# Differential attention with its units in twos, joint small steps, maxima written negated and lambda made in the query projection

## The chip, the cores and the metric

The kernel runs on one core of one Trainium2 chip. The metric is the device time of one execution in microseconds (us), the median over the runs. Five engines work side by side, each through its own queue of instructions in order: TensorE (PE in the profile, with its weight loads as PEld), VectorE (DVE), ScalarE (ACT), GpSimd (POOL) and SyncE (SP), which here issues the transfers. They wait for each other by semaphores, which the program writes out by hand.

## What is computed

The reference is two blocks of two layers each. The first has a convolution layer, a layer of differential attention, and a product-key expert layer behind each; the second has two attention layers of other kinds and two MLPs. The change touches the differential attention alone and the query projection ahead of it:

```python
def diff_attention(h, wq, k, v, lq1, lk1, lq2, lk2, subln_g, wo, lam_init, pos):
    q = (h @ wq).reshape(B, L, N_HEADS, 2, HEAD_DIM)
    q = partial_rope(q, pos) * (HEAD_DIM ** -0.5)
    lam = (jnp.exp(jnp.sum(lq1 * lk1)) - jnp.exp(jnp.sum(lq2 * lk2)) + lam_init)
    ...
        s = jnp.einsum('bqhcd,bkhcd->bhcqk', qblk, k).astype(jnp.float32)
        s = jnp.where(mask, s, -jnp.inf)
        p = jax.nn.softmax(s, axis=-1)
        a = p[:, :, 0] - lam * p[:, :, 1]
        return jnp.einsum('bhqk,bkhe->bqhe', a.astype(v.dtype), v)
    ...
    o = rmsnorm(o, subln_g) * (1.0 - lam_init)
    return o.reshape(B, L, N_HEADS * V_DIM) @ wo
```

There are 8 heads with two maps each, a head dimension of 64, values of 128, 256 tokens that ask (two tiles of 128) and 272 keys (16 meta tokens ahead of them). Each head's two score maps get a softmax of their own, and the second is subtracted with the factor lambda.

## The kernel before, in words

Matrix products in float32 precision are made from three products of rounded parts: the high part of the weights by the high part of x, high by low, low by high (`three`, L854). The weights stream from memory into a ring; ACT rounds them to a high part (`split_hi`, L546) and DVE makes the remainder (`split_lo`, L553), in halves of a chunk, four halves ahead of PE.

The stages follow each other in one list. Around the change these are `kv_proj`, `q_proj`, `diff_attn` and `proj_add`. In the query projection (8 chunks of 128 outputs, one for each head) PE projects chunk m and then multiplies the raw chunk m - 1 by a rotation matrix (`rotate`, L1231). ACT copies the raw chunk out of PSUM (L1882) and rounds the finished chunk m - 2 (`one`, L1890). DVE adds the sine part (L2569, L2571), POOL makes the cosine part (L3021) and the low part of the rounded chunk (L3027). Behind the last chunk ACT makes the two exponentials for lambda (`diff_lambda`, L1915) and DVE three small steps from them (L2605 to L2607).

The attention has 16 units u: token tile 0 with its 8 heads (144 keys), then tile 1 (272 keys). For a unit
- PE (`scores`, L1468, L1470) makes both score maps, six products and two for the causal mask, in banks 0 and 1 or 2 and 3;
- DVE (`maxima`, L2763, L2764) takes the row maxima and multiplies them by the negated scale;
- ACT (`exps`, L2058) makes both exponentials with row sums;
- DVE (`mix`, L2769 to L2773) makes reciprocals, the ratio, and the difference of the two maps;
- PE (`turn`, L1478) transposes the difference, ACT stores it (`store`, L2067), PE multiplies by the values (`weigh`, L1488) in bank 6 or 7;
- DVE (`keep_out`, L2779) scales and stores the output, ACT sums its squares (`square_sum`, L2074).

On each engine the steps of several units are interleaved in an order written out by hand: PE does `scores(u)`, `turn(u - 2)`, `weigh(u - 3)`, ACT `store(u - 2)`, `exps(u)`, `square_sum(u - 3)`, DVE `maxima(u)`, `mix(u - 1)`, `keep_out(u - 3)`. At the end ACT loads the table for the root and takes it (L1560, L2086), DVE inverts and scales the outputs (L2790, L2796), PE transposes them (L1509), and ACT and DVE make the high and low parts (L2089, L2800) that the output projection reads.

PE's clock is held up by products that nobody reads (`keep_warm`, L887): 20 ahead of the first scores and 6 behind each of the first three, 256 columns each. PE is given these by count, not by time. Which pattern of columns a call reads hangs on its count too: calls of 14 and of 20 products take the next pattern from a list that all later stages share.

Of the kernel before, what the change touches and what calls it, by code (L numbers as in the profile page):

```python
# [99 lines left out]
WARM_DIFF, WARM_FILL = 20, 6  # L100
# [94 lines left out]
def build_program(nc, dram, spill, meta_dram, out):  # L195
    stages = lay_out_stages()
    with ExitStack() as ctx:
# [148 lines left out]
        probs = av(3, 2, T0)  # L346
# [79 lines left out]
        row_max = small[:, 8:14].rearrange("p (a m) -> p a m", a=3)  # L426
        neg_max = small[:, 16:22].rearrange("p (a m) -> p a m", a=3)
        row_sum = small[:, 24:30].rearrange("p (a m) -> p a m", a=3)
# [421 lines left out]
        def _(pe):  # L850
# [29 lines left out]
            def keep_warm(n, bank=7):  # L880

                src = gated_all[:, 48:48 + SEQ]
                if n in (WARM_SCALE, WARM_DIFF):
                    parts, at = next(by_scale, (2, 48))
                    src = in_lines(at, parts)
# [570 lines left out]
            def attend_diff(s):  # L1456
# [17 lines left out]
                def turn(u):  # L1474
                    pe.wait_ge(maps_mixed, u + 1)
                    for kt, (k0, kn) in enumerate(diff_unit(u)[3]):
                        at = kt * P
                        mm = pe.transpose(banks[0:kn, 4 + u % 2, at:at + P], probs[:, u % 3, 0, k0:k0 + kn], ident)  # L1478
# [13 lines left out]
                keep_warm(WARM_DIFF)  # L1492
                pe.wait_ge(v_kept, NC)
                pe.wait_ge(masks_rounded, 1)
                for u in range(n_units + 3):
                    if u < n_units:
                        scores(u)
                    if u < 3:
                        keep_warm(WARM_FILL)
                    if 2 <= u < n_units + 2:  # L1500
                        turn(u - 2)
                    if u >= 3:
                        weigh(u - 3)
# [49 lines left out]
        def _(act):  # L1553
# [362 lines left out]

            def nsa_proj(s):
# [131 lines left out]
            def attend_diff(s):  # L2049
                n_units = NT * HEADS  # L2050

                def exps(u):
                    nk = diff_unit(u)[2]
                    act.wait_ge(max_ready, u + 1)
                    if u >= 3:
                        act.wait_ge(turned, u - 2)
                    for c in range(2):
                        ins = act.activation(probs[:, u % 3, c, 0:nk], banks[:, 2 * (u % 2) + c, 0:nk], ACT.Exp,  # L2058
                                             bias=neg_max[:, u % 3, c:c + 1], scale=SCALE, accum_out=row_sum[:, u % 3, c:c + 1])
# [16 lines left out]
                for u in range(n_units + 3):  # L2076
                    if 2 <= u < n_units + 2:
                        store(u - 2)
                    if u < n_units:
                        exps(u)  # L2080
# [1168 lines left out]
```

## Time and profile before

| | us |
|---|---|
| median of 3 runs | 2752.08 |
| lowest, highest | 2749.27, 2756.12 |
| the profiled execution | 2745.82 |
| its span, first to last instruction | 2744.0 |
| query projection, rotations of chunk 0 to the last | 1075 to 1099.6 |
| attention, first scores to output projection | 1102.4 to 1145.7 |

The page of the profile gives busy times, the granted clock of TensorE, the chain of work that ended last, and the costliest groups of instructions. The attention takes 43 us of 2744. So the page alone says little of it, and the views by stretch, by chain and by time are needed. The chain of waits follows, from the end backwards, what released each piece of work; a stretch in which it stays on one engine is bound by that engine. The granted clock is 1.00 at 2.4 GHz and 0.50 at 1.2 GHz.

### The profile page before, as it was taken

What the parts mean: (1) busy time and instruction counts of PE and PEld (TensorE: products, weight loads), DVE (VectorE), ACT (ScalarE), POOL (GpSimd) and SP (SyncE); (2) the same over time, 40 slices, a digit from 0 to 9 for tenths busy, and PEclk for the clock granted to TensorE, in tenths of its full rate; (3) what the DMA queues carried; (4) which work ended last, traced back from release to release, by engine and by line L of the source; (5) the groups of instructions that cost most, each with busy time, mean ns of one, the idle gap of its engine ahead of it and who ended that gap; (6) DMA issues with size and microseconds to landing.
All of it is one profiled execution on the core that took longest, in us unless ns stands there. A gap on an engine that the chain in (4) does not pass through costs nothing.

```text
span 2744.0 us, 60777 instructions
## 1 busy us (share of the span) xinstructions
PE 2674.1 (97%) x21677; PEld 2592.7 (94%) x21677; DVE 2037.2 (74%) x4473; ACT 1512.1 (55%) x3283; POOL 607.5 (22%) x655
## 2 busy tenths in 40 slices
PE   9999999999999999999999999999998999999998
PEld 9799989999999999899999999999987899988998
DVE  6769988787887867779888777777666766556665
ACT  6453455555555555652455555555555655556554
POOL 1034680021111204125850010010044400022000
PEclk9999999999999999999999999999999999999999
DMA  5045427787887855156347677676644056542564
GB/s 176 16 147 188 144 64 252 223 292 245 278 263 253 288 172 154 57 172 204 100 139 235 227 239 243 217 249 224 190 137 147 24 160 193 176 137 83 159 193 136
DMA packets 153655, 493.93 MB, mean 180 GB/s; under 512 B 18033, under 2 KB 37937, under 8 KB 153489
## 3 DMA queue, kind: packets, MB, share of 16 engines
q1 hardware_dynamic: 137424, 437.67, 49.0%
q0 software_dynamic: 15488, 54.11, 6.9%
q8 instruction: 93, 1.52, 0.2%
q14 instruction: 74, 0.60, 0.1%
q10 hardware_dynamic: 576, 0.03, 0.0%
HBM read 481.62 MB, written 10.13 MB: 179 GB/s over the span
## 4 chain that ended last, share of the span: by engine, by line
PE 87%; DVE 9%; ACT 2%; issue 1%; POOL 1%; DMA 1%; POOLq 0%; ACTq 0%; DVEq 0%
PE banks L854 68%; PE banks L1098 5%; PE banks L1119 3%; PE banks L996 2%; PE banks L892 1%; PE banks L1260 1%; PE banks L1411 1%; DVE meta_row L2404 1%; DVE work L2407 1%; PE banks L887 1%; DVE w_lo L553 1%; POOL x_lo L2915 1%; ACT w_hi L546 1%; PE banks L1381 1%; DVE arena L2346 1%
## 5 line engine op out<-in xcount | busy, mean ns | idle before, releaser
L553 DVE TENSOR_TENSOR w_lo<-ring,w_hi 128x512 fp32r<-128x512 f32 x1448 | 1014.8, 704 | 514.1 <-ACT w_hi L546 482.2
L546 ACT ACTIVATE w_hi<-ring 128x512 fp32r<-128x512 f32 x1448 | 908.7, 630 | 714.1 <-PE banks L854 692.3
L854 PE MATMUL banks<-gated_all,w_hi 128*128 128x240 f32 (+1 forms) x5120 | 877.5, 275 | 7.4 <-DVE gated_all L2471 7.3
L854 PE MATMUL banks<-x_hi,w_hi 128*128 128x240 f32 (+2 forms) x2752 | 774.2, 281 | 10.0 <-POOL x_lo L2915 6.3
L854 PEld LDWEIGHTS banks<-gated_all,w_hi 128*128 128x128 f32 x5120 | 770.2, 189 | 10.0 <-DVE gated_all L2471 10.0
L854 PE MATMUL banks<-x_lo,w_hi 128*128 128x240 f32 (+2 forms) x2752 | 764.1, 278 | 0.0
L854 PE MATMUL banks<-x_hi,w_lo 128*128 128x240 f32 (+2 forms) x2752 | 764.0, 278 | 0.0
L854 PE MATMUL banks<-gated_all,w_lo 128*128 128x240 f32 (+1 forms) x2560 | 702.7, 274 | 0.0
L854 PEld LDWEIGHTS banks<-x_hi,w_hi 128*128 128x128 f32 x2752 | 521.2, 189 | 21.1 <-issue 9.8
L854 PEld LDWEIGHTS banks<-x_lo,w_hi 128*128 128x128 f32 x2752 | 521.5, 189 | 0.4
L854 PEld LDWEIGHTS banks<-x_hi,w_lo 128*128 128x128 f32 x2752 | 520.9, 189 | 0.0
L854 PEld LDWEIGHTS banks<-gated_all,w_lo 128*128 128x128 f32 x2560 | 483.8, 189 | 0.0
L1098 PE MATMUL banks<-arena 128*128 128x240 f32 x1152 | 266.0, 366 | 0.0
L1098 PEld LDWEIGHTS banks<-arena 128*128 128x128 f32 x1152 | 203.8, 191 | 9.5
L3013 POOL TENSOR_SCALAR work<-const_a,pick 128x128 f32<-128x128 f32 x186 | 179.7, 977 | 36.8 <-PE banks L1119 36.1
L2967 POOL DMA_INDIRECT meta_row<-in_peer_u_rows,meta_expert x48 | 55.2, 1150 | 527.2 <-DVE meta_small L2435 516.0
L2468 DVE TENSOR_TENSOR work<-arena 128x240 f32<-128x240 f32 x256 | 153.6, 600 | 18.0 <-DMA arena<-spill 12.2
L1119 PEld LDWEIGHTS banks<-work,meta_row 128*128 128x128 f32 x960 | 137.6, 191 | 19.5 <-DVE work L2407 11.6
L1119 PE MATMUL banks<-work,meta_row 128*128 128x128 f32 x960 | 145.2, 278 | 6.9 <-DVE work L2407 4.1
L1742 ACT ACTIVATE arena<-banks 128x256 f32<-128x256 f32 x240 | 91.3, 383 | 100.5 <-PE banks L1119 92.8
L2471 DVE TENSOR_TENSOR gated_all<-work,gated_all 128x240 fp32r<-128x240 f32 (+1 forms) x320 | 130.0, 406 | 17.4 <-ACT gated_all L1828 15.2
L2967 POOL DMA_INDIRECT meta_row<-in_peer_v,meta_expert x48 | 54.6, 1138 | 391.7 <-DVE meta_x L2450 235.1
(386 smaller groups left out, 3216.0 us busy)
## 6 DMA issues: line engine op xcount, KB each, us to landing
ring<-in_peer_v SPq DMA_DIRECT2D x256, 512.0 KB, 3.6
ring<-in_peer_u SPq DMA_DIRECT2D x184, 512.0 KB, 4.6
arena<-in_peer_u SPq DMA_DIRECT2D x72, 512.0 KB, 3.6
ring<-in_mlp_up SPq DMA_DIRECT2D x64, 512.0 KB, 3.5
ring<-in_mlp_down SPq DMA_DIRECT2D x64, 512.0 KB, 3.5
ring<-w_peer_query SPq DMA_DIRECT2D x32, 512.0 KB, 3.5
ring<-w_fox_proj SPq DMA_DIRECT2D x24, 512.0 KB, 3.6
ring<-w_nsa_proj SPq DMA_DIRECT2D x20, 512.0 KB, 3.5
```

Of the source, the lines that this page charges most:

```text
L546: act.activation(w_hi[:, hn % SPLITS], raw_half(hn), ACT.Copy).then_inc(hi_ready, 1)
L553: dve.tensor_tensor(w_lo[:, hn % SPLITS], raw_half(hn), w_hi[:, hn % SPLITS].bitcast(F32), ALU.subtract)\
L854: mm = pe.matmul(out, w_at(w), x, start=start and j == 0, stop=stop and j == 2, skip_group_check=True)
L887: pe.matmul(banks[:, bank, 0:SEQ], gated_all[:, 0:P], src, start=True, stop=True)
L996: mm = pe.matmul(banks[:, tap_bank(c), 0:T0], diagonals[:, n], glu_u[:, c, w:w + T0], start=w == (SHARED_FROM if c == SHARED_CONV else 0), ...
L1098: mm = pe.matmul(banks[:, 6 + k % 2, 0:moved], early_ring[:, k % 4, c * P:(c + 1) * P], squares[:, c, tk_], start=c == 0, stop=c == NC - 1)
L1119: mm = pe.matmul(banks[:, g % 4, t * KEYS:(t + 1) * KEYS], onehot1[:, g % 4, t], onehot2[:, g % 4, t], start=True, stop=True)
L1742: act.activation(arena[:, 256 * g:256 * (g + 1)], banks[:, g % 4, 0:256], ACT.Copy).then_inc(spread_stored, 1)
L2468: dve.tensor_tensor(o, a, g, ALU.mult).then_inc(gated_f32_ready, 1)
L2471: dve.tensor_tensor(gated_lo[:, b, 0:tokens], act_gated[:, 0:tokens], gated_hi[:, b, 0:tokens].bitcast(F32), ALU.subtract).then_inc(gated_ ...
L2967: pool.indirect_dma_start(meta_row[:, g % 2], None, u if g < META_PICKS else v, bass.IndirectOffsetOnAxis(ap=meta_expert[:, o, j:j + 1], a ...
L3013: pool.tensor_scalar(onehot2[:, g % 4, 1], iota, pick[:, 1, at + 1:at + 2], pick[:, 2, at + 1:at + 2], ALU.is_equal, ALU.mult).then_inc(po ...
```

## The change

It does five things:
- lambda is made in the query projection: ACT's `diff_lambda` at chunk 2 (`query_beside`), DVE's three steps at chunk 5 (`keep_lambda`);
- the scale of the scores, 0.125, is put on the queries in the raw copy (`scaled=NC`), so that neither the exponential nor the maximum needs it; the maximum is written negated by the reduction itself;
- the units run in twos: each engine does a step for two units and then the next step for two others. Reciprocals, ratios and output scalings are one instruction for two units. `probs` and the small buffers have four places in place of three;
- the root table is loaded ahead of the last two stores, and the final transposes signal each bank;
- the 20 unread products ahead of the scores go, 12 stand behind each of the first two rounds of scores in place of 6 behind the first three units, and 18 on bank 4 stand between the last weighing and the final transposes.

```diff
 WARM_LAST_TAPS, WARM_CENTRE = 12, 9
-WARM_DIFF, WARM_FILL = 20, 6
...
-                if n in (WARM_SCALE, WARM_DIFF):
+                if n == WARM_SCALE:
                     parts, at = next(by_scale, (2, 48))
...
-                keep_warm(WARM_DIFF)
                 pe.wait_ge(v_kept, NC)
                 pe.wait_ge(masks_rounded, 1)
-                for u in range(n_units + 3):
-                    if u < n_units:
-                        scores(u)
-                    if u < 3:
-                        keep_warm(WARM_FILL)
-                    if 2 <= u < n_units + 2:
-                        turn(u - 2)
-                    if u >= 3:
-                        weigh(u - 3)
-                for half in range(2):
+                pairs = n_units // 2
+                scores(0)
+                scores(1)
+                for j in range(pairs + 2):
+                    if j < 2:
+                        keep_warm(2 * WARM_FILL)
+                    if j >= 2:
+                        weigh(2 * j - 4)
+                        weigh(2 * j - 3)
+                    for u in (2 * j, 2 * j + 1):
+                        if u + 2 < n_units:
+                            scores(u + 2)
+                        if 1 <= j <= pairs:
+                            turn(u - 2)
+                keep_warm(WARM_SUB, 4)
+                for b in range(4):
                     for t in range(NT):
-                        pe.wait_ge(sub_scaled, 2 * half + t + 1)
-                        for hd in range(4 * half, 4 * half + 4):
+                        pe.wait_ge(sub_scaled, 2 * (b // 2) + t + 1)
+                        for hd in (2 * b, 2 * b + 1):
                             at = (hd % 2) * SEQ + t * P
-                            mm = pe.transpose(banks[:, hd // 2, at:at + P], o_tok[:, t, hd * P:(hd + 1) * P], ident)
+                            mm = pe.transpose(banks[:, b, at:at + P], o_tok[:, t, hd * P:(hd + 1) * P], ident)
                     mm.then_inc(out_turned, 1)
...
+            def query_beside(m, one):
+                one(m - 2)
+                if m == 2:
+                    diff_lambda()
...
                     act.wait_ge(max_ready, u + 1)
-                    if u >= 3:
-                        act.wait_ge(turned, u - 2)
+                    if u >= 4:
+                        act.wait_ge(turned, u - 3)
                     for c in range(2):
-                        ins = act.activation(probs[:, u % 3, c, 0:nk], banks[:, 2 * (u % 2) + c, 0:nk], ACT.Exp,
-                                             bias=neg_max[:, u % 3, c:c + 1], scale=SCALE, accum_out=row_sum[:, u % 3, c:c + 1])
+                        ins = act.activation(probs[:, u % 4, c, 0:nk], banks[:, 2 * (u % 2) + c, 0:nk], ACT.Exp,
+                                             bias=neg_max[:, u % 4, c:c + 1], accum_out=row_sum[:, u % 4, c:c + 1])
...
-                    if u == n_units:
+                pairs = n_units // 2
+                for j in range(pairs + 2):
+                    if j < pairs:
+                        exps(2 * j)
+                        exps(2 * j + 1)
+                    if j == pairs:
                         load_root_table()
-                    if u >= 3:
-                        square_sum(u - 3)
+                    if 1 <= j <= pairs:
+                        store(2 * j - 2)
+                        store(2 * j - 1)
+                    if j >= 2:
+                        square_sum(2 * j - 4)
+                        square_sum(2 * j - 3)
...
                 for b in range(4):
-                    act.wait_ge(out_turned, b // 2 + 1)
+                    act.wait_ge(out_turned, b + 1)
...
-                    rope(s, s["n0"], 8, SEQ, beside=lambda m, one=one: one(m - 2))
+                    rope(s, s["n0"], 8, SEQ, beside=lambda m, one=one: query_beside(m, one), scaled=NC)
                     one(6)
                     one(7)
-                    diff_lambda()
...
+            def keep_lambda():
+                dve.wait_ge(lam_steps, 2)
+                steps.link(dve.tensor_tensor(neg_lam, lam_exp[:, 1:2], lam_exp[:, 0:1], ALU.subtract))
+                steps.link(dve.tensor_scalar(neg_lam, neg_lam, -LAM_INIT, None, ALU.add))
+                steps.link(dve.tensor_scalar(subln_gain, subln_gain, 1.0 - LAM_INIT, None, ALU.mult))
...
-                steps.link(dve.tensor_tensor(neg_lam, lam_exp[:, 1:2], lam_exp[:, 0:1], ALU.subtract))
-                steps.link(dve.tensor_scalar(neg_lam, neg_lam, -LAM_INIT, None, ALU.add))
-                steps.link(dve.tensor_scalar(subln_gain, subln_gain, 1.0 - LAM_INIT, None, ALU.mult))
+                     beside=lambda m: keep_values(NC - 1) if m == 0 else keep_lambda() if m == 5 else None)
...
-                    steps.link(dve.reduce_max(row_max[:, u % 3], banks[:, 2 * (u % 2):2 * (u % 2) + 2, 0:nk], AX_X))
-                    dve.tensor_scalar(neg_max[:, u % 3], row_max[:, u % 3], -SCALE, None, ALU.mult).then_inc(max_ready, 1)
+                    dve.tensor_reduce(neg_max[:, u % 4], banks[:, 2 * (u % 2):2 * (u % 2) + 2, 0:nk], AX_X, ALU.max, negate=True)\
+                       .then_inc(max_ready, 1)
                 def mix(u):
                     nk = diff_unit(u)[2]
-                    dve.wait_ge(exp_done, u + 1)
-                    steps.link(dve.reciprocal(recips[:, u], row_sum[:, u % 3]))
-                    steps.link(dve.tensor_scalar(ratios[:, u:u + 1], recips[:, u, 1:2], row_sum[:, u % 3, 0:1], neg_lam,
-                                                 ALU.mult, ALU.mult))
-                    first, second = (probs[:, u % 3, c, 0:nk] for c in range(2))
-                    dve.scalar_tensor_tensor(out=first, in0=second, scalar=ratios[:, u:u + 1], in1=first,
-                                             op0=ALU.mult, op1=ALU.add).then_inc(maps_mixed, 1)
+                    both = slice(u % 4, u % 4 + 2)
+                    dve.wait_ge(exp_done, u + 2)
+                    steps.link(dve.reciprocal(recips[:, u:u + 2], row_sum[:, both]))
+                    steps.link(dve.scalar_tensor_tensor(out=ratios[:, u:u + 2], in0=recips[:, u:u + 2, 1], scalar=neg_lam,
+                                                        in1=row_sum[:, both, 0], op0=ALU.mult, op1=ALU.mult))
+                    for i in range(2):
+                        first, second = (probs[:, (u + i) % 4, c, 0:nk] for c in range(2))
+                        dve.scalar_tensor_tensor(out=first, in0=second, scalar=ratios[:, u + i:u + i + 1], in1=first,
+                                                 op0=ALU.mult, op1=ALU.add).then_inc(maps_mixed, 1)
                 def keep_out(u):
                     t, hd = diff_unit(u)[0:2]
-                    dve.wait_ge(av_done, u + 1)
-                    dve.tensor_scalar(o_tok[:, t, hd * P:(hd + 1) * P], banks[:, 6 + u % 2, 0:P], recips[:, u, 0:1], None, ALU.mult)\
-                       .then_inc(o_kept, 1)
-
-                for u in range(n_units + 3):
-                    if u < n_units:
-                        maxima(u)
-                    if 1 <= u < n_units + 1:
-                        mix(u - 1)
-                    if u >= 3:
-                        keep_out(u - 3)
+                    dve.wait_ge(av_done, u + 2)
+                    dve.tensor_tensor(o_tok[:, t, hd * P:(hd + 2) * P].rearrange("p (i e) -> p i e", i=2), banks[:, 6:8, 0:P],
+                                      recips[:, u:u + 2, 0:1].broadcast_to([P, 2, P]), ALU.mult).then_inc(o_kept, 2)
+
+                pairs = n_units // 2
+                for j in range(pairs + 2):
+                    if j < pairs:
+                        maxima(2 * j)
+                        maxima(2 * j + 1)
+                    if 1 <= j <= pairs:
+                        mix(2 * j - 2)
+                    if j >= 2:
+                        keep_out(2 * j - 4)
```

## Rows read from the trace of the kernel before

**Rows 1.** The page: busy time of the engines, and the chain by engine
```profile
PE 2674.1 (97%) x21677; PEld 2592.7 (94%) x21677; DVE 2037.2 (74%) x4473; ACT 1512.1 (55%) x3283; POOL 607.5 (22%) x655
PE 87%; DVE 9%; ACT 2%; issue 1%; POOL 1%; DMA 1%; POOLq 0%; ACTq 0%; DVEq 0%
```
**Rows 2.** Busy time by stretch: stretch, us, then busy us of PE, PEld, DVE, ACT, POOL, clock
```profile
1110.00:1134.00 24.00, 24.00 (x183) 18.95 (x182) 21.57 (x70) 20.71 (x84) 0.00 (x0) 1.00 0.01 2
```
**Rows 3.** Chain of waits, middle of the attention: start us, us, what
```profile
1113.79 0.58 PE banks L1468 x6
1114.37 0.44 PE banks L1470 x2
1114.81 0.22 PE banks L1478 x2
1115.03 0.64 PE banks L1488 x4
...
1128.96 0.33 PE banks L1478 x3
1129.29 0.86 PE banks L1488 x6
```
**Rows 4.** Chain of waits, head of the attention
```profile
1101.46 0.51 DVE arena L2571
...
1102.43 1.28 ACT L1915
...
1103.72 0.21 ACT small L1915
...
1104.53 0.47 DVE small L2763
...
1105.22 0.84 ACT arena L2058 x4
```
**Rows 5.** Chain of waits, tail of the attention
```profile
1133.39 0.74 DVE small L2763
...
1135.98 0.40 issue
...
1140.15 0.41 ACT arena L2074 x2
...
1141.21 0.70 DVE arena L2796
...
1141.96 3.67 PE banks L1509 x16
...
1145.71 14.32 PE banks L854 x120
```
**Rows 6.** Busy time by stretch, the granted clock behind the count of POOL
```profile
120.00:140.00 20.00, 17.03 (x98) 14.92 (x97) 8.84 (x18) 12.10 (x28) 6.08 (x8) 0.91 0.00 1
400.00:420.00 20.00, 17.50 (x143) 16.39 (x143) 12.25 (x29) 9.33 (x21) 9.95 (x11) 1.00 0.49 156
1140.00:1141.00 1.00, 0.00 (x0) 0.00 (x0) 0.19 (x2) 0.71 (x3) 0.00 (x0) 0.50 0.00 0
```
**Rows 7.** Timeline of ACT and PE, chunk 2 of the query projection: start us, us, what
```profile
1085.59 0.40 ACT L1890 ACTIVATE q_hi<-arena 128x256 fp32r<-128x256 f32 x1
1085.90 0.36 ACT L1882 ACTIVATE arena<-banks 128x256 f32<-128x256 f32 x1
1088.06 0.59 PE L1231 MATMUL banks<-arena 128*128 128x256 f32 x2
```
**Rows 8.** Timeline, single small steps of the attention and a first product behind it
```profile
1112.47 0.35 DVE L2779 TENSOR_SCALAR arena<-banks,arena 128x128 f32<-128x128 f32 x1
1113.19 0.38 ACT L2067 ACTIVATE arena<-banks 128x256 f32<-128x256 f32 x1
1113.46 0.17 DVE L2764 TENSOR_SCALAR small<-small 128x2 f32<-128x2 f32 x1
1146.06 0.42 PE L854 MATMUL banks<-x_lo,w_hi 128*128 128x256 f32 x1
```

More of the change, by code:

```diff
@@ L99 @@
 WARM_LAST_TAPS, WARM_CENTRE = 12, 9
-WARM_DIFF, WARM_FILL = 20, 6
+WARM_SUB, WARM_FILL = 18, 6
 EXPS_BEFORE = {11: 0, 19: 1, 21: 2}
@@ L345, in build_program @@
         ratios = av(2 * HEADS)
-        probs = av(3, 2, T0)
+        probs = av(4, 2, T0)
         o_tok = av(NT, D)
@@ L425, in build_program @@
         lam_sum, lam_exp, neg_lam = small[:, 2:4], small[:, 4:6], small[:, 6:7]
-        row_max = small[:, 8:14].rearrange("p (a m) -> p a m", a=3)
-        neg_max = small[:, 16:22].rearrange("p (a m) -> p a m", a=3)
-        row_sum = small[:, 24:30].rearrange("p (a m) -> p a m", a=3)
+        neg_max = small[:, 16:24].rearrange("p (a m) -> p a m", a=4)
+        row_sum = small[:, 24:32].rearrange("p (a m) -> p a m", a=4)
         sub_ss, sub_root, sub_rstd = (small[:, 44 + 16 * i:60 + 16 * i] for i in range(3))
@@ L1477, in turn @@
                         at = kt * P
-                        mm = pe.transpose(banks[0:kn, 4 + u % 2, at:at + P], probs[:, u % 3, 0, k0:k0 + kn], ident)
+                        mm = pe.transpose(banks[0:kn, 4 + u % 2, at:at + P], probs[:, u % 4, 0, k0:k0 + kn], ident)
                     mm.then_inc(turned, 1)
@@ L2074, in square_sum @@
                     act.activation(square_out, o_tok[:, t, hd * P:(hd + 1) * P], ACT.Square, accum_out=sub_ss[:, u:u + 1]).then_inc(sub_squared, 1)
-                for u in range(n_units + 3):
-                    if 2 <= u < n_units + 2:
-                        store(u - 2)
-                    if u < n_units:
-                        exps(u)
-                    if u == n_units:
-                        load_root_table()
-                    if u >= 3:
-                        square_sum(u - 3)
+                pairs = n_units // 2
[4 more added lines that the diff above has]
+                    if j == pairs:
+                        load_root_table()
+                    if 1 <= j <= pairs:
[4 more added lines that the diff above has]
+                        square_sum(2 * j - 3)
                 act.wait_ge(sub_squared, n_units)
@@ L2602, in q_proj @@
                 rope(s, 8, SEQ, lambda m: diff_rope_dst(NC + m), set_b["rope_sin"][:, META:T0],
-                     beside=lambda m: keep_values(NC - 1) if m == 0 else None)
-                dve.wait_ge(lam_steps, 2)
-                steps.link(dve.tensor_tensor(neg_lam, lam_exp[:, 1:2], lam_exp[:, 0:1], ALU.subtract))
-                steps.link(dve.tensor_scalar(neg_lam, neg_lam, -LAM_INIT, None, ALU.add))
-                steps.link(dve.tensor_scalar(subln_gain, subln_gain, 1.0 - LAM_INIT, None, ALU.mult))
+                     beside=lambda m: keep_values(NC - 1) if m == 0 else keep_lambda() if m == 5 else None)
             def nsa_proj(s):
@@ L2776, in keep_out @@
                 def keep_out(u):
                     t, hd = diff_unit(u)[0:2]
-                    dve.wait_ge(av_done, u + 1)
-                    dve.tensor_scalar(o_tok[:, t, hd * P:(hd + 1) * P], banks[:, 6 + u % 2, 0:P], recips[:, u, 0:1], None, ALU.mult)\
-                       .then_inc(o_kept, 1)
-                for u in range(n_units + 3):
-                    if u < n_units:
-                        maxima(u)
-                    if 1 <= u < n_units + 1:
-                        mix(u - 1)
-                    if u >= 3:
-                        keep_out(u - 3)
+                    dve.wait_ge(av_done, u + 2)
```

## Prediction

> **What bounds the kernel now.** I read the page first. TensorE (PE) is busy for 97% of the span and carries 87% of the chain that ended last [rows 1]. What the other engines spend counts only where PE waits for them. The change touches the last part of the query projection and the differential attention, so I went next to busy time by stretch. In the 24 us in the middle of the attention PE is busy for all 24.00, VectorE (DVE) for 21.57 and ScalarE (ACT) for 20.71 [rows 2]. The chain of waits over the same stretch gives the price of a unit. Of a unit of the first token tile PE spends 0.58 us on six score products, 0.44 on the two mask products, 0.22 on two turns and 0.64 on four weighing products, together about 1.87. Of the second tile it spends 1.02 on scores and mask, 0.33 on turns and 0.86 on weighing, together 2.2 [rows 3]. The units before follow each other at exactly that distance, so in the middle the many small DVE steps are hidden behind PE.
>
> Two places are not. At the head of the stage the chain leaves PE. DVE ends the last rope addition at 1101.97, ACT then loads the Exp table (1.28 us) for lambda, DVE waits for that and makes three small steps, and the first maximum starts only at 1104.53. The first Exp follows at 1105.22 [rows 4]. At the tail (from the last scores at 1133.37 to the output projection at 1145.71) the chain runs through ACT and DVE: root table, store, weigh, keep, square, root, reciprocal, scaling, and then 16 turns at 0.23 us each, twice the 0.11 of the same turns in the middle (two in 0.22) [rows 3, 5], because the granted clock is 0.50 from 1140 on [rows 6]. That is 1.2 GHz in place of 2.4.
>
> So the stage can give or take a few microseconds of 2744, whatever the edits remove.
>
> **Part 1: lambda in the query projection.** The Exp and its table load move to chunk 2 of the projection, between the rounding of chunk 0 (L1890, 1085.59) and the raw copy of chunk 2 (L1882, 1085.90, 0.36 us), both on ACT [rows 7]. They cost 1.28 + 0.01 + 0.21 = 1.50 us there. The raw copy then ends at about 1087.8. What needs it first is PE's rotation of chunk 2, issued at 1088.06 [rows 7], so 0.2 to 0.3 us of cover is left and the move costs nothing. If the cover is gone, PE stands still for the excess, us for us. Queued behind it on ACT is the split of the next weight half; four halves are split ahead, and PE needs one in some 1.4 us, so that isn't late. Later copies on ACT need no load of their own: the copies between the Exps have none today. DVE's three small steps (0.17 each with issue) move to chunk 5, into idle time before a rotation. No DMA moves. Scaling the queries by 0.125 in the raw copy is free, since that copy has a scale operand today.
>
> At the head, what is late next is the rope chain itself: its last addition ends at 1101.97 before and after, since DVE's two weight splits and the rope are ahead of it. The 20 warm products in front of the scores go, so scores 0 and 1 are done by about 1101.9. The first maximum starts at 1102.0 and the negated form needs no second step (0.17): Exps of unit 0 start at 1102.5 in place of 1105.22. **Gain 2.7 us at the head.** In the ramp up to the scores of unit 6, PE has 4 scores, 12 warm products (1.4), 2 turns and 2 weighings, 7.1 us in place of 7.6 (4 scores, 6 warm products, 4 turns, 3 weighings). Another 0.4 is gained there, and the work not done yet comes later.
>
> **Part 2: maxima negated, and joint small steps.** Sixteen negations of 0.17 us go [rows 8]. Sixteen reciprocals and ratios become eight, and 16 output scalings of 0.35 [rows 8] become eight of twice the width, which I take as between 0.35 (one) and 0.70 (two). DVE gets some 0.3 us a unit lighter. PE was full and DVE had slack already, so all of this is worth nothing in the middle. At the tail one unit's steps are on the path.
>
> **Part 3: the order in twos.** This is what costs. ACT's order in a round is now: Exps of both units, store of both turned maps, square sums of two older units. The second store waits for the last instruction of PE's round, the second turn. Behind it on ACT are queued the two square sums and then the Exps of the next round, and PE's next scores wait for those, as they reuse the banks. Between a round's last turn and the next scores PE has only its two weighings to do. In the first tile ACT needs 0.38 (store [rows 8]) + 2 x 0.41 (squares [rows 5]) + 0.84 (Exps [rows 4]), less two overlaps of 0.09 (the copy at 1085.90 starts 0.09 before the rounding ahead of it ends [rows 7]) and plus 0.1 for hand-overs: 1.95. The weighings are 2 x 0.64 = 1.28. PE waits 0.67. Where the Exps are of the second tile they take some 0.22 more and PE waits 0.89, in two rounds; where the store and the weighings are of the second tile as well it waits 2.28 - 1.72 = 0.56. The rounds with older squares in front of Exps and scores behind them are four (Exps of units 6, 8, 10, 12): 0.67 + 2 x 0.89 + 0.56 = **3.0 us lost in the body**. Before, a store was followed by Exps that PE had a whole unit of work to cover. The scores of unit 15 then end at about 1131.5, against 1133.37: of the 3.1 gained, 1.9 is left, and more turns and weighings are still to do.
>
> **Part 4: the tail.** I count from the last turn of that round, at 1131.8. ACT: Exps 14 end at +2.3, Exps 15 at +3.2, two stores +4.0, two squares +4.8, the root table and its first root 1.5 (as at the head, 1.28 + 0.21) +6.2, store 14 +6.6. In the kernel before the table came after store 14, now it is in front of stores 14 and 15, and PE waits for them. PE: two weighings of 0.86, +8.3. DVE's joint output +8.9, two squares +9.8, root and reciprocal +10.5. The scaling starts at 1142.3, and did at 1141.21 [rows 5]. **The tail is 3.0 us longer, counted from the last scores** (10.8 against 7.8).
>
> The 18 warm products on bank 4 follow the last weighing and are meant for the clock. Whether they find it whole is the open point. Before, the clock was down by 1140, 6.6 us after the last scores [rows 5, 6], with only turns and weighings in between. In the new order the last weighing ends 8.7 us after the last scores, with longer idle times. I therefore take the clock as down in it. The last two weighings then cost 0.8 more (12 products at 0.23 against 0.16), the scaling starts at 1143.1, and 18 products of 256 columns at half clock (0.21 each, twice the 0.11 of their fast pace) take 3.8 us and end at 1144.8, where the first turn is wanted at 1143.8. They do bring the clock back during the turns, and these run as the scaled quarters come. The last bank's turns end at +14.8, and the first bank's high part and remainder (0.63 and 0.7) at +15.05: the projection starts at 1146.9, against 1145.71. Its first products were at half clock before (0.42 in place of 0.28 at 1146.06 [rows 8]), some 0.4 us altogether, which now go. Sum: 1146.9 - 1145.71 - 0.4 = **+0.8 us**.
>
> From there on PE is the bound again and passes any shift on unchanged. The profiled execution took 2745.82 (span 2744.0), the median of the runs shown is 2752.08, and these runs lie between 2749.27 and 2756.12. The sum of +0.8 is made in the profiled execution and put on the median: 2752.9. A measurement of this kernel can tell about 0.3% (8 us) from no change; the whole stage's edits move less than that.
>
> **The rivals.** (A) The clock stays whole in the tail. For it: PE still has some work in every two microseconds, and the warm products come directly behind it. Then the scaling starts at 1142.3, the turns take 1.8 in place of 3.7 and the projection starts 3.25 after it, 1145.6: -0.1 - 0.4 = -0.5, so 2751.6. (B) The round trip over ACT is covered, because the operations overlap more than I allow or the square sums find their outputs late and ACT isn't slowed by them. Against it: the order in the program is strict. Then the body keeps PE's pace and 3.0 of the loss go: 2749.9, and 2748.6 with the clock whole. (C) Slower: the idle times in the body (3.0 of 21 us, PE 86% busy) bring the clock down there. The place is PE's queue in units 6 to 15, the price twice the time of each product: PE has 18 us of work in it, of which a quarter to all may be run at half clock, +4 to +18, so 2757 to 2771. It decides from the point at which PE's share in the body is too low to keep 1.00. The stretch from 400 to 420 has PE busy for 17.50 of 20 at 1.00, that from 120 to 140 for 17.03 of 20 at 0.91 [rows 6]: the body lies between them, but with gaps of under a microsecond each. (D) The table load drags more with it than its own 1.28. The chain shows 0.01 us between load and Exp at the head [rows 4], but 0.40 of nothing before the load in the tail [rows 5]. With 0.40 more the raw copy ends at 1088.2 and PE waits 0.1, nothing to see: 2753.0.
>
> The Trainium skill (ScalarE: Activation LUTs, What ACT_TABLE_LOAD costs) puts a switch of tables at about 1.28 us for the load and 1.38 more to drain. The trace agrees on the load and not on the drain, as the Exp started 0.01 us after it. By that page the raw copy of chunk 2 would end at 1089.2 and PE would stand for 1.1 us in the projection, a total of 2754.0.
>
> **How the numbers follow.** Forecast (stall in the body, clock down only in the tail) 0.45; A 0.22; B 0.20; C 0.08; D 0.05. Four of the five lie between 2748.6 and 2753.0. The low end comes from B less 2 us of spread between runs, the high end from the low part of C and the same spread: 2746.5 to 2758.5; what is left out is most of C and a spread of medians beyond the one shown. Faster by over 0.3% would need 8 us, more than the whole head and tail can give, so only the spread can do it: 0.03. Slower by over 0.3% is the upper half of C and the spread: 0.06. Within 0.3%: 0.91.
>
> **What would show it.** The first Exp of the attention 2.5 to 3 us earlier after the last rope addition, with no table load in front. PE's chain in the body showing waits of 0.5 to 0.9 us for ACT's Exps once a round, four times; none would be B. The scores of unit 15 about 1.9 us earlier and the scaling 1 to 2 us later. In the tail, the granted clock at the warm products: 0.50 for the forecast, 1.00 for A. The raw copy of chunk 2 ending before PE's rotation; a wait of PE there is D. A clock below 1.00 in the body is C. I am wrong if the stage as a whole moves by more than 4 us.

## The result and the profile after

The changed kernel takes 2755.95 us (median of 20 runs, 2749.55 to 2767.79), the kernel before 2747.87 beside it (20 runs, 2738.93 to 2765.42): a ratio of 1.003, 95% interval 1.0019 to 1.0042, or 8 us more. The profiled execution of the changed kernel took 2764.08, with a span of 2762.2, so it is one of the longer ones. The mean granted clock over the 20 runs is 0.9886; in the kernel before it was 0.9916 over 35 runs taken beside the first experiments. The share of the span at 1.2 GHz is twice what is missing to 1, so that is 63 us at half clock against 46.

The page hardly shows it. Busy time of the engines and chain by engine:

```profile
PE 2691.9 (97%) x21681; PEld 2607.7 (94%) x21681; DVE 2031.2 (74%) x4433; ACT 1511.6 (55%) x3283; POOL 608.4 (22%) x655
PE 86%; DVE 10%; ACT 2%; issue 1%; POOL 1%; DMA 0%; POOLq 0%; ACTq 0%; DVEq 0%
```

PE is busy for 18 us more than in [rows 1] with four products more. The attention by stretch (stretch, us, then busy us of PE, PEld, DVE, ACT, POOL, and the granted clock) tells why:

```profile
1102.00:1112.00 10.00, 10.00 (x77) 7.77 (x76) 5.47 (x18) 4.95 (x22) 0.00 (x0) 1.00 0.01 3
1112.00:1122.00 10.00, 9.49 (x48) 6.90 (x48) 4.56 (x11) 5.57 (x25) 0.00 (x0) 0.63 0.00 1
1122.00:1132.00 10.00, 10.00 (x45) 7.44 (x41) 4.89 (x12) 4.57 (x20) 0.00 (x0) 0.52 0.01 2
1132.00:1142.00 10.00, 9.10 (x63) 7.03 (x63) 5.30 (x14) 8.37 (x31) 0.00 (x0) 1.00 0.00 0
1142.00:1153.00 11.00, 11.00 (x50) 9.62 (x48) 3.93 (x8) 4.11 (x15) 0.00 (x0) 0.54 0.00 0
```

Against the 1.00 of [rows 2], the clock is near 0.50 for 17 us in the body and for 10 us in the tail. In the second stretch PE starts 48 products where the first had 77.

The chain of waits (start us, us, what) at the head, the counterpart of [rows 4]:

```profile
1099.52 0.52 DVE arena L2583
...
1100.06 0.43 ACT q_hi L1894
...
1100.56 0.73 POOL q_lo L3045
...
1101.41 0.64 PE banks L1467 x6
```

The Exp table and lambda's steps are gone from it. The chain of the first round in which PE waits, and the next ones:

```profile
1111.06 0.23 PE banks L1477 x2
...
1111.32 0.38 ACT arena L2076
1111.70 0.30 ACT arena L2083 x2
...
1112.39 0.38 ACT arena L2067 x2
...
1113.26 0.64 PE banks L1467 x4
...
1114.56 0.90 PE banks L1467 x6
...
1116.61 2.60 PE banks L1487 x8
...
1133.12 0.58 PE banks L1467 x6
```

From a round's last turn the chain goes to ACT: the store, two square sums (L2083), the Exps (L2067), and back to PE's next scores at 1113.26, 1.97 us after the turn ended. From 1114.56 on the same six score products take 0.90 and then 0.98 in place of 0.57, and eight weighing products 2.60 in place of 1.47. From there the chain is on PE alone until 1135: at half clock PE is slower than ACT's trip, and nobody waits for ACT any more.

The tail, beside [rows 5]:

```profile
1146.50 4.14 PE banks L886 x18
1150.64 2.55 PE banks L1513 x16
...
1153.28 11.83 PE banks L853 x101
```

I measure the stage from the start of the last rope addition to the first product of the output projection, by the chain. Before it is 1145.71 - 1101.46 = 44.3 us, after 1153.28 - 1099.52 = 53.8.

### The profile page after: what moved, and what is told of

Same layout as the page of the kernel before. It is cut to its first block, busy times and chain, and to the rows that moved or that the text cites. A ratio compares the mean times of both kernels' runs of the same rounds, so it can differ in the third digit from the quotient of the medians.

```text
span 2762.2 us, 60752 instructions
## 1 busy us (share of the span) xinstructions
PE 2691.9 (97%) x21681; PEld 2607.7 (94%) x21681; DVE 2031.2 (74%) x4433; ACT 1511.6 (55%) x3283; POOL 608.4 (22%) x655
## 4 chain that ended last, share of the span: by engine, by line
PE 86%; DVE 10%; ACT 2%; issue 1%; POOL 1%; DMA 0%; POOLq 0%; ACTq 0%; DVEq 0%
PE banks L853 68%; PE banks L1097 5%; PE banks L1118 2%; PE banks L995 2%; DVE meta_row L2416 1%; DVE work L2419 1%; PE banks L886 1%; PE banks L891 1%; PE banks L1410 1%; PE banks L1259 1%; DVE w_lo L552 1%; PE banks L1380 1%; POOL x_lo L2933 1%; ACT w_hi L545 1%; DVE arena L2358 1%
## 5 line engine op out<-in xcount | busy, mean ns | idle before, releaser
L853 PE MATMUL banks<-x_hi,w_hi 128*128 128x240 f32 (+2 forms) x2752 | 775.2, 282 | 10.7 <-POOL x_lo L2933 7.5
```

The costliest lines, as they stand in the source:

```text
L853: mm = pe.matmul(out, w_at(w), x, start=start and j == 0, stop=stop and j == 2, skip_group_check=True)
```

## The experiments

All ran beside the kernel before. Each group of four experiments shares 35 runs of it, so a ratio has an interval of about 0.2% to either side. The totals alone can't separate 3 us; the profiles can, but are one execution each. Stage and half clock in this table are from the profiled execution, the mean clock from 12 runs (20 for the changed kernel; for the kernel before from the 35 runs of each of the three groups). "Scores of unit 15" below are counted by the start of their last product, from the start of the last rope addition.

| kernel | ratio to before | 95% interval | stage, us | of it at half clock | mean clock |
|---|---|---|---|---|---|
| before | 1 | | 44.3 | 5.9 | 0.9916, 0.9916, 0.9913 |
| changed | 1.003 | 1.0019 to 1.0042 | 53.8 | 27.3 | 0.9886 |
| e1_squares_first | 1.0016 | 0.9998 to 1.0034 | 47.9 | 13.7 | 0.9914 |
| e2_fill | 1.0011 | 0.9989 to 1.0033 | 47.6 | 0 | 0.9928 |
| e3_head_alone | 1.0003 | 0.9987 to 1.0019 | 41.1 | 2.3 | 0.9917 |
| e4_pattern | 1.0034 | 1.0009 to 1.0059 | 47.1 | 3.4 | 0.9905 |
| e5_ones_slowed | 0.9998 | 0.998 to 1.0016 | 44.2 | 5.4 | 0.9908 |
| e6_twos_alone | 1.0039 | 1.002 to 1.0057 | 54.3 | 20.5 | 0.9891 |
| e7_no_tail_products | 1.0043 | 1.0024 to 1.0061 | 47.7 | 9.5 | 0.9882 |
| e8_root_between | 1.0034 | 1.0015 to 1.0054 | 55.0 | 27.3 | 0.9897 |
| e9_ones_waiting | 1.0005 | 0.9984 to 1.0026 | 48.4 | 11.8 | 0.9894 |
| e10_ones_rest | 0.9979 | 0.9962 to 0.9996 | 40.7 | 3.4 | 0.9919 |
| e11_ones_tail | 0.9988 | 0.9968 to 1.0008 | 40.0 | 0 | 0.9925 |
| e12_twos_mended | 1.0013 | 0.9994 to 1.0033 | 43.9 | 0 | 0.9923 |

Theory C: the round trip over ACT makes PE wait, and by that the clock falls in the body. Rival L: the loss lies behind the attention. Rival O: the order in twos lets the clock fall by itself.

**e1_squares_first.** In the changed kernel, on ACT:

```diff
+                    if 2 <= j < pairs:
+                        square_sum(2 * j - 4)
+                        square_sum(2 * j - 3)
                     if 1 <= j <= pairs:
                         store(2 * j - 2)
                         store(2 * j - 1)
-                    if j >= 2:
+                    if j >= pairs:
```

> The changed kernel with one thing moved on ACT: in the rounds that still have Exps ahead, the two square sums stand in front of the two stores and not behind them. Theory C (the round trip over ACT makes PE wait, the clock falls in the body and stays at 1.2 GHz): the trip gets 0.8 us shorter, 1.1 us against 1.28 of weighing, PE doesn't wait, the granted clock stays 1.00 from the first scores to the scores of unit 15, and the attention from the last rope addition to the output projection takes 42 to 44 us in place of 53. Total about 9 us below the changed kernel, 0.1% below to 0.1% above the kernel before. Rival L (the loss lies behind the attention, in the pace of later products): the attention gets 3 us shorter at most, the total stays 0.2 to 0.3% above the kernel before.

Its body by stretch, then its tail, and below the chain of a round and of the start of the tail:

```profile
1112.00:1122.00 10.00, 10.00 (x76) 7.30 (x75) 7.12 (x17) 8.21 (x37) 0.00 (x0) 1.00 0.01 2
...
1131.00:1145.00 14.00, 13.79 (x53) 11.48 (x54) 3.84 (x8) 4.82 (x15) 0.00 (x0) 0.51 0.00 0
```

```profile
1118.68 1.47 PE banks L1487 x8
1120.14 0.58 PE banks L1467 x6
...
1129.43 0.44 DVE arena L2798
...
1129.89 0.41 ACT arena L2083 x2
...
1131.21 3.71 PE banks L1487 x12
```

Scores follow the weighings without a wait, the clock is 1.00 in the whole body, and the last product of the scores of unit 15 starts 27.7 us after the start of the last rope addition, against 35.7. The body did what theory C asks. The stage did not: 47.9 in place of 42 to 44. In round 7 I had put the square sums ahead of the stores too, where they wait for DVE's output (L2798), which waits for the weighing: PE stands until 1131.21, the clock falls there, and the tail takes 15.2 us from that last score product to the reciprocal. The mean clock is back at the 0.9914 of the kernel before.

**e2_fill.** In the changed kernel, on PE, behind the two weighings of a round:

```diff
+                    if 2 <= j < pairs:
+                        keep_warm(WARM_FILL, 4)
```

> The changed kernel with 6 unread products (0.7 us at 2.4 GHz) on bank 4 behind the two weighings of rounds 2 to 7, where PE waits for ACT's Exps. The waits themselves stay. Theory C, and within it that it is PE's idle time or too few products that let the clock fall: the clock stays 1.00 in the body, the waits are covered by the products, and the attention takes 44 to 46 us; total 7 us below the changed kernel. If the clock falls all the same, the order of the real products is what lets it fall and the products cost up to 1.4 us a round at half clock: 8 us above the changed kernel. Rival L: total unchanged within 1 us.

```profile
1111.65 1.47 PE banks L1487 x8
1113.12 0.90 PE banks L886 x6
1114.02 0.58 PE banks L1467 x6
```

```profile
1110.00:1120.00 10.00, 10.00 (x74) 7.49 (x73) 5.25 (x15) 6.23 (x28) 0.00 (x0) 1.00 0.00 1
1120.00:1130.00 10.00, 10.00 (x74) 7.92 (x74) 6.00 (x14) 6.87 (x28) 0.00 (x0) 1.00 0.01 2
```

The chain is now filled by the unread products, the clock is 1.00 through the whole stage, and the mean clock of the runs is above that of the kernel before. The stage is 47.6, over the 44 to 46 expected, and part of that is the filling itself: it takes 0.9 us in each of rounds 2 to 6, where e4 below waits for 0, 0.5, 0.7, 0.7 and 0.3 us. By the scores of unit 15 that is 2.1 us (32.2 here, 30.1 in e4 without its short fall of the clock). Its total (1.0011) can't be told from no change.

**e3_head_alone.** In the kernel before: `query_beside` and `keep_lambda` as in the change, and `keep_warm(WARM_DIFF)` left out.

> The kernel before with lambda made in the query projection and the 20 products ahead of the scores left out (the pattern that they took from the list is still taken), all else as before. My prediction's part 1: Exps of unit 0 start 0.5 to 0.7 us after the last rope addition in place of 3.2, the middle keeps its pace of 1.87 and 2.20 us a unit at a clock of 1.00, attention 41 us in place of 43.7, total 2.7 us (0.1%) below the kernel before. If missing products at the head let the clock fall in the body, the attention is longer than 43.7, and the order in twos is not needed for the loss.

The stage is 41.1 as expected, the body at 1.00, the first Exp 1.1 us behind the start of the last rope addition in place of 3.8. The total shows no gain (1.0003), though -0.12% lies within its interval. Whether something outside the stage takes it back, these runs can't tell.

**e4_pattern.** In the changed kernel `next(by_scale)` ahead of the scores, nothing else.

> The changed kernel, but the pattern that the 20 products took from the shared list is still taken, so that all later calls read the columns that they read in the kernel before. Theory C: no difference from the changed kernel, 0.3% above the kernel before, the clock at 0.50 in the body as there. Rival L in the form that the shifted patterns slow or cool what comes later: the total falls by 3 us or more, and the stages behind the attention take as long as in the kernel before.

The total is where the changed kernel's is and not 3 us lower, so nothing speaks for the shifted patterns, L in this form; its interval is too wide to rule it out alone. As PE's work in the stage is the same as in the changed kernel, this profile is in effect a second look at it, and it differs:

```profile
1112.00:1122.00 10.00, 8.77 (x64) 6.52 (x62) 5.59 (x15) 6.23 (x28) 0.00 (x0) 1.00 0.00 1
1122.00:1132.00 10.00, 8.97 (x55) 6.59 (x54) 5.42 (x14) 6.49 (x27) 0.00 (x0) 0.83 0.01 2
```

The same waits (PE idle for 12% and 10% here), but the clock is down for only 3.4 us in the body, and the stage takes 47.1. I had expected 0.50 as in the other profile: the waits make the fall possible, not certain, and how long it lasts varies from execution to execution. In the five profiles with the unmended order it is down in the body for 17, 3, 10, 3 and 26 us (changed, e4, e6, e7, e8). In each of them it falls 0.1 to 1.4 us behind the end of one of these waits: the first, 0.5 us long, in the changed kernel and e8, the second in e6, the third in e4 and e7.

**e5_ones_slowed and e9_ones_waiting.** In e3_head_alone, on ACT behind the Exps of units 6 to 15, two extra copies, in e9 three (the diff is e9's, behind the Exps):

```diff
+                    if 6 <= u < n_units:
+                        steps.link(act.activation(raw[:, 0, 0:T0], set_b["rope_cos"], ACT.Copy))
+                        steps.link(act.activation(raw[:, 1, 0:P], set_b["rope_cos"][:, 0:P], ACT.Copy))
+                        steps.link(act.activation(raw[:, 0, 0:P], set_b["rope_cos"][:, 0:P], ACT.Copy))
```

> The kernel before, in its order of single units, with lambda in the query projection as in e3_head_alone, and behind the Exps of units 6 to 15 two extra copies on ACT (272 and 128 elements, to places that nobody reads in this stage), some 0.75 us a unit. ACT then needs 2.3 us a unit in the first tile and 2.6 in the second, against PE's 1.87 and 2.20: PE waits about 0.4 us a unit, 0.8 in two, as much as in the order in twos. Theory C in the form that idle time of PE in the body lets the clock fall, whatever the order: the granted clock falls to 0.50 between units 6 and 15 and stays down for several us, and from the last rope addition to the output projection it takes 50 us or more (41.1 in e3_head_alone). Rival O (it is the order in twos, with longer runs of thin products behind each other, that lets it fall): the clock stays 1.00 through the body and the stage takes 45 to 46 us, the waits alone.

> As e5_ones_slowed, which made a unit of the second tile only 2.41 us long in place of 2.20, with a third extra copy on ACT (272, 128 and 128 elements) behind the Exps of units 6 to 15. A unit then takes 2.3 to 2.4 us in the first tile and 2.7 to 2.8 in the second, and PE is idle for a fifth of the body, more than the seventh that it was in the order in twos. Theory C (idle time in the body lets the clock fall, in any order): in the runs as a whole the mean granted clock is 0.989 or lower (0.9916 in the kernel before), in the profile it is 0.50 for some us within the body, and the total is 6 to 12 us above the kernel before. Rival O (the order in twos itself): the clock stays 1.00 in the body, the mean is 0.991 or more, and the total is 3 to 4 us above the kernel before (waits 5 us, tail 1 us, head -2.7).

ACT had more room than I reckoned. In e5 the scores of unit 15 start only 0.6 us later than in e3; they add no wait of PE to the body, and it tells nothing. In e9 they start 3.0 us later, and the body by stretch is

```profile
1117.00:1127.00 10.00, 9.82 (x70) 6.99 (x68) 8.51 (x29) 9.56 (x40) 0.00 (x0) 1.00 0.00 1
1127.00:1137.00 10.00, 9.14 (x61) 6.33 (x60) 7.47 (x22) 9.69 (x38) 0.00 (x0) 1.00 0.01 2
```

PE is idle for 2% and 9%, still less than in e4, in waits of 0.2 us each at most against 0.5 to 0.7 there, and the clock holds in the body. It fell in the tail, for 11.8 us. The mean clock (0.9894) is as theory C had it, the total (1.0005) as rival O. Undecided: whether waits as long as those of the order in twos bring the clock down in the order of single units was not shown. That the mean over 12 runs went from 0.9917 in e3 to 0.9894 speaks for it, but the one profile has the fall in the tail alone, where the copies lengthen the waits too.

**e6_twos_alone.** The changed kernel with lambda, its three steps and the 20 products back where they were.

> The changed kernel with its part 1 taken back: lambda's Exp and table load behind the query projection, DVE's three steps there too, and the 20 products ahead of the scores. Order in twos, negated maxima and joint steps stay. My account: the head is 2.5 to 2.7 us longer than in the changed kernel and nothing else changes; total 0.3 to 0.5% above the kernel before. If the missing 20 products were what lets the clock fall, it stays 1.00 in the body and the stage takes 47 us (4 us of it the head).

The first Exp is 2.7 us later again, the clock is down in the body all the same, and the total is 1.0039. So the missing 20 products are not the cause.

**e7_no_tail_products.** The changed kernel without `keep_warm(WARM_SUB, 4)`.

> The changed kernel without the 18 unread products between the last weighing and the final turns. Where the clock is down in the tail, they took 4.1 us of the chain, ending 1.3 us after the first scaled quarter; without them the turns start with the scaled quarters, at half clock or at full. Account: the first turn follows the start of the reciprocal by 1.0 us in every run in place of 1.0 to 2.1, the 16 turns take 3.7 us at half clock in place of 2.6, and the projection starts within 1 us of where it does now: no difference in the total. If the products do harm, total 1 us or more below the changed kernel.

The 16 turns took 3.85 us at half clock, the first 1.0 us behind the start of the reciprocal, the stage 47.7 beside e4's 47.1. In these profiles the 18 products neither help nor harm by more than that.

**e8_root_between.** The changed kernel with `load_root_table()` behind the two stores.

> The changed kernel with the root table loaded behind the stores of units 14 and 15 and not ahead of them. My prediction's part 4: the load (1.5 us with its root) is on the path of the last stores. Moved behind them, it lies beside the last two weighings on PE: the scaling starts 1.2 to 1.5 us earlier, counted from the last scores (10.2 in place of 11.5 at full clock). If the load isn't on the path, nothing moves. Total: 1.3 us below the changed kernel, less than the runs can tell.

The first and the last line of the chain's stretch from the weighings of units 12 and 13 to the reciprocal, in e8_root_between and then in e2_fill, where the table is ahead of the stores (both at 1.00):

```profile
1149.99 2.18 PE banks L1487 x12
...
1157.25 0.27 DVE small L2808
```

```profile
1135.51 2.18 PE banks L1487 x12
...
1142.76 0.27 DVE small L2810
```

7.26 and 7.25 us: the place of the load makes no difference. The table is not on the path.

**e10_ones_rest and e11_ones_tail.** The kernel before with all of the change but the order in twos, the joint steps and the tail products: e3_head_alone and

```diff
-                    steps.link(dve.reduce_max(row_max[:, u % 3], banks[:, 2 * (u % 2):2 * (u % 2) + 2, 0:nk], AX_X))
-                    dve.tensor_scalar(neg_max[:, u % 3], row_max[:, u % 3], -SCALE, None, ALU.mult).then_inc(max_ready, 1)
+                    dve.tensor_reduce(neg_max[:, u % 3], banks[:, 2 * (u % 2):2 * (u % 2) + 2, 0:nk], AX_X, ALU.max, negate=True)\
+                       .then_inc(max_ready, 1)
```

with the queries scaled and a signal for each bank of the final turns. e11 adds `keep_warm(12, 4)` behind the last weighing.

> Everything of the change but the order in twos, the joint steps and the tail products: lambda in the query projection, no products ahead of the scores, queries scaled, maxima written negated, a signal for each bank of the final turns; single units in the order of the kernel before. Account: the head as in e3_head_alone (-2.7), the middle at PE's pace at 1.00, one negation less at head and tail (-0.3), turns by bank let the projection start 0.3 to 1 us earlier. Stage 40 to 41 us from the last rope addition to the projection (44.3 before, 41.1 in e3_head_alone), total 0.1% below the kernel before. If the negated maximum or the rest costs anything, the stage is over 41.1.

> e10_ones_rest with 12 unread products on bank 4 between the last weighing and the final turns. PE is idle there for 2.2 us. If the clock is whole when they start, they end before the first scaled quarter and keep it: turns in 1.8 to 2.6 us in place of 3.7 and the stage 1 us shorter than in e10. If it has fallen they take 2.6 us and delay the first turn by 0.3 us: the stage is as long as in e10 or 0.3 longer. I expect the second, since the clock was down by 0.2 us after the last weighing in the kernel before.

e10 is faster than the kernel before, 0.9979 with an interval below 1, and by that faster than the changed kernel. Its profile gives 3.6 us of the 5.8; the rest is not accounted for, and an interval that ends at 0.9996 is a narrow one among thirteen comparisons. Its tail by the chain:

```profile
1139.31 1.14 PE banks L1488 x6
...
1141.64 0.26 DVE small L2796
...
1142.67 3.47 PE banks L1509 x16
1146.15 1.37 PE banks L854 x12
```

The turns are still at half clock. In e11 the clock stayed 1.00 in the stage, which I had not expected, and that was worth 0.7 us of it; its total can't be told from e10's.

**e12_twos_mended.** The changed kernel with the square sums ahead in rounds 2 to 6 only, the root table behind the stores, and 6 unread products in rounds 7 and 8.

> The changed kernel in its order in twos with three mends on ACT and PE: square sums ahead of the stores in rounds 2 to 6 only, the root table behind the last stores, and 6 unread products behind the weighings of rounds 7 and 8. Theory C: the body runs without waits at 1.00 (scores of unit 15 start 27.7 us after the last rope addition, as in e1_squares_first), the tail is 10 to 11 us at full clock, and the stage takes 41 to 43 us: total within 0.1% of the kernel before, 6 us below the changed kernel. If the clock still falls in the tail, the stage takes 46 us.

The clock is 1.00 through the stage and the body has no waits. The stage takes 43.9, just over the range I gave, and the total (1.0013) can't be told from no change. The order in twos can be mended, but even so it is 3.2 us longer than single units in e10; 1.8 us of its chain are the added unread products.

## Why the prediction was right, and where not

The measured time lies in the range (2746.5 to 2758.5), but near its upper end. The likeliest case, +0.8 us, was not what happened, and that the time lies in the range is in part luck. The forecast stood on 2752.08, the median of three runs; over 20 runs the kernel before takes 2747.87. The measured +8 us on 2752.08 would be 2760.2, above the range. By my own sign (wrong if the stage moves by more than 4 us) the mechanism was wrong: the stage is 9.5 us longer in the profile. Point by point:

- **Head.** Right. The first Exp starts 0.9 us behind the start of the last rope addition, against 3.8 before: 2.85 us gained, 2.7 forecast.
- **Lambda in the projection.** Right. On ACT's timeline of chunk 2

```profile
1080.07 1.28 ACT L1919 ACT_TABLE_LOAD   x1
1081.36 0.20 ACT L1919 ACTIVATE small<-small 128x2 f32<-128x2 f32 x1
1081.47 0.37 ACT L1886 ACTIVATE arena<-banks 128x256 f32<-128x256 f32 x1
```

  the raw copy ends 1.77 us after the load began, as [rows 4, 7] gave, and chunk 3 follows with no delay on ACT. The load starts 0.02 us after the rounding ahead of it ends, so rival D is out. The further 1.38 us of the Trainium skill (ScalarE: Activation LUTs, What ACT_TABLE_LOAD costs) do not appear between load and Exp here, as in the kernel before.
- **DVE's lighter steps.** Worth nothing in the middle, as forecast.
- **The round trip over ACT.** Right in its place and its size: 1.97 us from the last turn to the next scores, 1.95 forecast. Two weighings in a row took 1.47, not twice 0.64, so PE waits 0.5 of it, not 0.67. The round is as long as I said. All four waits can be seen only where the clock is nearly whole (e4): 0.5, 0.7, 0.7 and 0.3, together 2.3 us against 3.0. There the last product of unit 15's scores starts at 31.8 us, of which 1.7 is the short fall: 30.1, against 29.8 by the prediction's 1131.5, which is that product's end.
- **The tail.** 11.5 us from the last score product to the reciprocal in e4 and e2, where my steps give 10.7. The mis-sized term is the weighing: two units back to back took 2.18 in the tail, and I charged twice 0.86, in two places. That the root table is on the path was wrong by e8; the weighings cover it.
- **The clock.** This is the step that failed: the forecast charged the waits at their own length and let the clock be whole in the body. I set case C (a fall in the body) at 0.08, because gaps under a microsecond, at a PE share of 86%, seemed too short. I compared with two stretches of other work, one at 1.00 with PE busy for 88% and one at 0.91 with 85% [rows 6], and such a share over 20 us decided nothing here: e4 has 88% and 90% in its two stretches of 10 us, and 1.00 and 0.83. It fell in all five profiles of the unmended order, for 3 to 26 us. C's own price was right: +4 to +18 us, measured +8.

The sum closes within the intervals. At 1.00 the changed order costs about 1.2 us more than the kernel before (e4's 47.1 less the 1.7 of its short fall, against 44.3). The runs of the changed kernel and of e4, e6, e7 and e8, which keep its order, have a mean clock of 0.9882 to 0.9905, against 0.9916: 6 to 19 us more at half clock, 3 to 9 us lost. By each kernel's own mean clock that gives 9, 4, 11, 11 and 6 us (changed, e4, e6 with its longer head, e7, e8), and their ratios say 8, 9, 11, 12 and 9, each to within 3 to 7 us either way. Taking the waits away (e1) or filling them (e2) brings the mean clock back and half to two thirds of the lost time with it, as far as totals with such intervals tell; e4 moves later patterns and brings nothing. That the waits in the order in twos cause the loss of clock in the body is shown by e1, e2 and e12 together: it held through the body in all three profiles without the waits, and fell in all five with them. Whether the same waits would do it in another order stays open, by e9.

## What to carry to other kernels

A wait of half a microsecond in a stretch where PE is the bound costs its own length only as long as the clock holds; ahead of an edit to the order, follow the last instruction of each round on PE through the other engines' queues, and see what is queued ahead of the step that lets PE go on. Small steps with slack (square sums here) belong where their engine waits anyway, not between a store and the Exps that PE waits for. Of a change in many parts, time the parts: here one part lost more than all others gained, and the others without it (e10) measured 0.2% faster than the kernel before.

## What the hardware showed that I had not expected

Once down, the clock stays down although PE has no idle time: from 1115 to 1131 PE is busy for all of each microsecond and granted 0.50, in work that held 1.00 for 24 us in [rows 2]; in e8 it stays down for 27 us. In the changed kernel it rises at 1131.7 with PE as busy as before, and no run shows what it rises for.

Weighing products of two units behind each other take longer than of one (1.47 for eight against 0.64 for four; against 0.86 for six, 1.92 for twelve in the body of e1 and 2.18 in the tail). No run here tells why.

The pace of the same products isn't fixed at full clock. The chain in the last stage, in the kernel before and then in the changed one:

```profile
2599.91 40.12 PE banks L854 x354
```

```profile
2613.89 40.16 PE banks L853 x341
```

One product in 0.113 us there, in 0.118 here, with nothing else on the chain, the granted clock at 1.00, and no part of the change near. The last 1440 such products take 163.5 us in one pace and 169.9 in the other, 6.4 us more. It isn't the order of the units: of the six profiles with single units four have the first and two the second, of the eight in twos four and four. Other stretches vary in pace too, in different places in different profiles. It accounts for a good part of why the profiled execution is 18 us longer and the stage only 9.5. That it is a part of the spread between runs of one kernel is likely, not shown; what sets it was not tried.
